# Hybrid decoder step on one core: the order of decode's loads on the SP queue

## The chip, the cores and the metric

The kernel runs on one core of a Trainium2 chip. The metric is the device time of one execution in microseconds (us); times of several executions are given by their median. The profiled execution is one more execution, recorded with a trace.

## The reference

One layer of a decoder is applied to a prompt of 512 tokens and to a decode batch of 8 sequences with 4 new tokens each. Each sequence of the decode batch has 1024 past tokens in a paged cache of 8 pages of 128 rows, found through `page_table`.

```python
yp, nsa_p, diff_p, win_p = decoder_layer(yp, p_nsa0, p_diff0, p_win0, ...)        # prompt
s_nsa  = cache_nsa_kv[l][page_table].reshape(DB, past_len, 4, 4, 64)              # k_cmp, v_cmp, k_sel, v_sel
s_diff = cache_diff_kv[l][page_table].reshape(DB, past_len, 2, 8, 128)            # keys (k1|k2), values
ys, nsa_s, diff_s, win_s = decoder_layer(ys, s_nsa, s_diff, s_win, ...)           # decode

# decoder_layer
proj = rmsnorm(x) @ w_in
o_a = nsa_mixer(...)     # 16 heads: compressed, selected and sliding branches, gated per head
a   = masked_softmax(q1 k1 + bias) - lam * masked_softmax(q2 k2 + bias)           # 8 heads
o_b = rmsnorm(a @ v) * (1 - lam_init)
h = x + (sigmoid(ga) * o_a + sigmoid(gb) * o_b) @ w_o
y = h + square(relu(rmsnorm(h) @ w_up)) @ w_down
```

## The kernel before

The program runs through five stages, each in a block of its own: projection, compression, prompt attention, decode attention (`decode_attention`, about 1008 to 1290 us in the trace) and the output projection with the MLP (`finish`). The change is in the loads of decode attention, and in the few of them that are issued while prompt attention still runs.

**Rounds.** Decode attention takes the 8 sequences in four rounds, `i` = 0 to 3 (`PAIRS` = 4), two sequences (a pair) in each. In a round TensorE (PE) turns key pages by transposes (`turn`), VectorE (DVE) or ScalarE (ACT) copies them out of PSUM into one of four slots, and PE multiplies them with the queries (`multiply`). `decode_steps` writes this order out as a list of steps. For a round it is: compressed keys (`cmp`), new rows, selected-branch pages (`sel`, 0 to 5), in rounds 1 to 3 the difference-attention values of the round before (`p_dif`, `p_dif_n`), `sel` 6 and 7, window pages (`win`), key pages of the difference attention (`dif`, each page k has four steps) 0 and 1, the values of the other branches (`p_sel`, `p_few`, `p_win`), and `dif` pages 2 to 7. In the last round all eight `dif` pages come ahead of the values. The values of the last round, `p_dif`, end the stage. So a value page of round i is read by PE some 10 us into round i + 1, while the list's key pages 4 to 7 are read at the end of round i. The list itself is not changed.

**Loads.** All large loads are issued by SP, in the order of its program, into one queue which the 16 DMA engines work off. SP also waits in that order: a wait in its program holds up all that stands behind it. For a pair there are, for both sequences together:

- `sel_load`: 8 pages, 2 x 256 KB each, into `big`. It waits until `nsa_mm` says that the values of the round before have been read
- `win_load`: 4 x 2 x 256 KB
- `key_load` (L204): 8 pages `dk`, 2 x 512 KB each, into four buffers (`KEY_PAGES`). Page k of round i goes where page k - 4 was, so `load_k` waits until the last of that page's four turns has been made (`turned`). The buffer of pages 0 and 4 is named `all_dk` in the profile, the others `de_dk`
- `load_v` (L1778): 8 pages `dv`, 2 x 512 KB each, into one buffer of eight pages. There is no second buffer, so round i's may be written only when PE has read round i - 1's
- `load_new` (L1765 to L1773), `pair_rows` (L177 to L179) and `dv_n` (L1797): new rows, compressed values `vc`, `gates`, queries and the like, together about 0.5 MB.

A page's place in the cache is a number in the table. `page_values` (L183) reads it into a register of SP: 16 reads for a pair. `sel`, `win` and the first `dk` page of pair 0 are loaded during prompt attention, which waits for `combined` before it may write `big` (L191).

Of the kernel before, what the change touches and what calls it, by code (L numbers as in the profile page):

```python
# [28 lines left out]
DEC_B, DEC_T = 8, 4  # L29
# [4 lines left out]
N_PAGES = PAST // PAGE  # L34
# [118 lines left out]
KEY_PAGES, KEYS_AHEAD = 4, 1  # L153
# [945 lines left out]
def prompt_attention(nc, d, shared):  # L1099


    with ExitStack() as ctx:
        s = Space(nc, ctx, "pa")
# [139 lines left out]
        def _(sp):  # L1243
# [28 lines left out]
            pages = page_values(sp, d, shared, 0)  # L1272

            sp.wait_ge(combined, NH)
            sel_load(sp, d, shared, pages, range(N_PAGES))
            win_load(sp, d, shared, 0)
            for k in range(KEYS_AHEAD):
                key_load(sp, d, shared, pages, 0, k)
# [349 lines left out]
def decode_attention(nc, d, shared):  # L1628


    with ExitStack() as ctx:
# [42 lines left out]
            shared.q_in, shared.kc_in, shared.sel_in, shared.win_in, shared.dk_in, shared.consts_in)  # L1674
        dv_in = [s.sem(f"dv_in{k}") for k in range(N_PAGES)]
# [85 lines left out]
        def _(sp):  # L1761
            def load_new(i):
# [5 lines left out]
                sp.dma_start(dk_n, split(d["diff_s"][new, 0:1024])).then_inc(new_in, 16)  # L1768
                sp.dma_start(vc[:], d["vc_s"][P * i:P * (i + 1), :]).then_inc(new_v_in, 16)
# [5 lines left out]

            def load_v(pages, i, k):
                for b in range(2):
                    sp.dma_start(dv[:, b, k, :], d["cache_diff"][bass.ds(pages[b][k], 1), :, 1024:2048]  # L1778
                                 .rearrange("n p e -> (n p) e")).then_inc(dv_in[k], 16)
# [9 lines left out]
            pages = page_values(sp, d, shared, 0)  # L1789
            for k in range(KEYS_AHEAD, KEY_PAGES):  # L1790
                load_k(pages, 0, k)
            for i in range(PAIRS):
                last = i + 1 == PAIRS
                if i:
                    sp.wait_ge(diff_mm, i)
                new = slice(2 * DEC_T * i, 2 * DEC_T * (i + 1))
                sp.dma_start(dv_n, d["diff_s"][new, 1024:2048].rearrange("(b t) e -> t b e", b=2)).then_inc(dv_n_in, 16)  # L1797
                load_v(pages, i, 0)
                load_v(pages, i, 1)
                if not last:  # L1800

                    sp.wait_ge(q_turned, i + 1)
                    sp.wait_ge(turned, AT[i, "cmp", 0, 0] + 1)
                    pair_rows(sp, d, shared, i + 1)
                load_v(pages, i, 2)
                load_v(pages, i, 3)
                load_k(pages, i, 4)
                load_v(pages, i, 4)
                load_k(pages, i, 5)
                load_v(pages, i, 5)  # L1810
                if not last:
                    following = page_values(sp, d, shared, i + 1)
                    sp.wait_ge(nsa_mm, i + 1)
                    sel_load(sp, d, shared, following, range(0, 3))
                    load_new(i + 1)
                load_k(pages, i, 6)
                if not last:
                    sel_load(sp, d, shared, following, range(3, 6))
                load_k(pages, i, 7)
                if not last:  # L1820
                    sel_load(sp, d, shared, following, range(6, 8))
                load_v(pages, i, 6)
                load_v(pages, i, 7)
                if not last:
                    win_load(sp, d, shared, i + 1)
                    for k in range(KEY_PAGES):
                        load_k(following, i + 1, k)
                    pages = following
# [22 lines left out]
        def _(pe):  # L1851
# [60 lines left out]
            def multiply(g):  # L1912
# [64 lines left out]
                elif kind == "p_dif":  # L1977
                    if i:
                        pe.wait_ge(diff_read, i)
                    for x in range(N_PAGES):  # L1980
                        pe.wait_ge(dv_in[x], 32 * i + 32)
                        for b in range(2):
                            for half in range(2):
                                o = 64 * b + 32 * half
                                ins = pe.matmul(ps_d[o:o + 32, :], tile[:, 64 * x + 32 * b:64 * x + 32 * b + 32],
                                                dv[:, b, x, CW * half:CW * (half + 1)], start=x == 0, stop=False)
                else:
# [820 lines left out]
```

## Time and profile before

| | us |
|---|---|
| three runs, median | 1776.53 |
| three runs, lowest and highest | 1768.65, 1789.45 |
| profiled execution, time | 1771.22 |
| profiled execution, span of the trace | 1769.4 |

The span runs from the first to the last instruction of the core; 1.8 us lie around it. Over the span PE is busy 92% of the time, DVE 45%, ACT 33% and GpSimd (POOL) 6%, and the mean granted clock of TensorE is 0.963 of full speed. The loads move 265.7 MB. Since the stages differ, the shares of the span say little about the loads of one of them; the rows further down are of the stage that the change touches.

### The profile page before, as it was taken

The page shows a single profiled execution, that of the slowest core. Times are in us where ns is not written, and L with a number is a line of the kernel's source. Part 1 is how long each engine was busy: PE and PEld are TensorE (multiplying, and loading weights), DVE is VectorE, ACT ScalarE, POOL GpSimd, SP SyncE. Part 2 cuts the span into 40 slices and gives each one's busy share as a digit, 9 for nine tenths or more (in the row PEclk, how much of TensorE's full clock was granted, in tenths as well). Part 3 has the DMA queues.
Part 4 walks back from the last instruction along what each step waited for, and adds up shares of the span by engine and source line. Part 5 has one row for each costly group of instructions (what it writes and reads, how often), then busy time and mean ns, then how long its engine had stood idle before and what let it go on. Part 6 is the DMA issues. An engine that isn't in the chain of part 4 may idle for free. (4 is left out here: it accounts for less than half of the span.)

```text
span 1769.4 us, 32753 instructions
## 1 busy us (share of the span) xinstructions
PE 1634.7 (92%) x12968; PEld 1360.4 (77%) x12968; DVE 804.9 (45%) x1873; ACT 586.8 (33%) x1236; POOL 106.0 (6%) x194
## 2 busy tenths in 40 slices
PE   7999999997899996788999888998979999999997
PEld 4888888775688885567777665765667999999997
DVE  4576633114233335867666544443454442234322
ACT  4232212222233324656555332332333332123210
POOL 0000000000000000035422100000000000000000
PEclk9999999998899998999999898998989999999999
DMA  8745555242532035542231089999842343333321
GB/s 279 294 163 169 161 162 161 91 137 51 137 78 73 8 97 151 140 145 69 89 116 31 17 322 361 364 337 341 325 159 72 95 132 111 113 115 121 97 71 51
DMA packets 187903, 265.71 MB, mean 150 GB/s; under 512 B 35261, under 2 KB 115517, under 8 KB 187654
## 3 DMA queue, kind: packets, MB, share of 16 engines
q1 hardware_dynamic: 183750, 244.31, 42.7%
q10 hardware_dynamic: 3136, 11.22, 1.7%
q0 software_dynamic: 896, 8.56, 1.4%
q8 instruction: 76, 1.25, 0.3%
q14 instruction: 45, 0.37, 0.1%
HBM read 240.98 MB, written 42.60 MB: 160 GB/s over the span
## 5 line engine op out<-in xcount | busy, mean ns | idle before, releaser
L614 PE MATMUL pj_ps<-all_hi,pj_xh 128*128 128x512 f32 x480 | 191.1, 398 | 1.5 <-DVE all_lo L508 1.5
L616 PE MATMUL pj_ps<-all_hi,pj_xl 128*128 128x512 f32 x480 | 189.5, 395 | 0.0
L615 PE MATMUL pj_ps<-all_lo,pj_xh 128*128 128x512 f32 x480 | 189.4, 395 | 0.0
L1424 ACT ACTIVATE pa_sc<-pa_sc,pa_nmax 128x32 f32<-128x32 f32 (+4 forms) x256 | 126.0, 493 | 115.0 <-DVE pa_nmax L1473 114.6
L2669 PE MATMUL fi_ps<-fi_fl,fi_wh 128*128 128x272 f32 x512 | 149.4, 292 | 0.0
L2670 PE MATMUL fi_ps<-fi_th,fi_wl 128*128 128x272 f32 x512 | 148.3, 290 | 0.0
L2670 PE MATMUL fi_ps<-fi_fh,fi_wl 128*128 128x272 f32 x512 | 148.3, 290 | 0.0
L2668 PE MATMUL fi_ps<-fi_th,fi_wh 128*128 128x272 f32 x512 | 147.6, 288 | 0.7 <-DVE fi_tl L2470 0.7
L2668 PE MATMUL fi_ps<-fi_fh,fi_wh 128*128 128x272 f32 x512 | 148.2, 289 | 0.0
L2669 PE MATMUL fi_ps<-fi_tl,fi_wh 128*128 128x272 f32 x512 | 147.2, 287 | 0.0
L2053 ACT ACTIVATE de_slot<-de_ps_t 128x512 f32<-128x512 f32 (+5 forms) x124 | 62.9, 514 | 188.1 <-PE de_ps_t L1888 98.4
L2165 DVE COPY de_slot<-de_ps_t 128x512 f32<-128x512 f32 (+4 forms) x112 | 68.8, 623 | 116.7 <-PE de_ps_t L1888 71.3
L1387 PE MATMUL pa_ps_t<-all_ident,pa_sc 128*128 128x128 f32 (+1 forms) x464 | 77.5, 285 | 36.0 <-DVE pa_keys L1481 12.6
L614 PEld LDWEIGHTS pj_ps<-all_hi,pj_xh 128*128 128x128 f32 x480 | 90.3, 188 | 25.4 <-issue 2.8
L1016 PE MATMUL cm_ph<-cm_xh,all_hi 128*128 128x512 f32 x256 | 108.4, 424 | 0.2 <-DVE cm_xl L880 0.2
L616 PEld LDWEIGHTS pj_ps<-all_hi,pj_xl 128*128 128x128 f32 x480 | 90.3, 188 | 21.4
L615 PEld LDWEIGHTS pj_ps<-all_lo,pj_xh 128*128 128x128 f32 x480 | 90.3, 188 | 20.8
L2396 ACT ACTIVATE fi_wh<-all_big 128x2048 fp32r<-128x2048 f32 x30 | 57.3, 1909 | 138.5 <-PE fi_ps L2670 138.5
L1017 PE MATMUL cm_ph<-cm_xl,all_hi 128*128 128x512 f32 x256 | 101.7, 397 | 0.0
L1018 PE MATMUL cm_ph<-cm_xh,all_lo 128*128 128x512 f32 x256 | 101.5, 396 | 0.0
L2668 PEld LDWEIGHTS fi_ps<-fi_fh,fi_wh 128*128 128x128 f32 x512 | 97.3, 190 | 0.0
L2670 PEld LDWEIGHTS fi_ps<-fi_fh,fi_wl 128*128 128x128 f32 x512 | 97.1, 190 | 0.0
(319 smaller groups left out, 3191.2 us busy)
## 6 DMA issues: line engine op xcount, KB each, us to landing
de_dv<-in_cache_diff SPq DMA_DIRECT2D x64, 512.0 KB, 10.5
all_big<-in_w_in SPq DMA_DIRECT2D x14, 2048.0 KB, 8.3
all_big<-in_cache_nsa SPq DMA_DIRECT2D x96, 256.0 KB, 5.6
de_dk<-in_cache_diff SPq DMA_DIRECT2D x48, 512.0 KB, 10.2
all_big<-in_w_up SPq DMA_DIRECT2D x16, 1024.0 KB, 5.5
all_big<-in_w_down SPq DMA_DIRECT2D x16, 1024.0 KB, 6.1
all_first<-in_cache_nsa SPq DMA_DIRECT2D x32, 256.0 KB
all_win<-in_cache_win SPq DMA_DIRECT2D x32, 256.0 KB, 10.7
```

The costliest lines, as they stand in the source:

```text
L614: pe.matmul(ps[:, t, :], xh[:, k, xk], hi(k), start=k == 0, stop=False)
L615: pe.matmul(ps[:, t, :], xh[:, k, xk], lo(k), start=False, stop=False)
L616: ins = pe.matmul(ps[:, t, :], xl[:, k, xk], hi(k), start=False, stop=k == KT - 1)
L1016: pe.matmul(o, w1h[k][:, kt, col], mh, start=first, stop=False)
L1017: pe.matmul(o, w1h[k][:, kt, col], ml, start=False, stop=False)
L1018: ins = pe.matmul(o, w1l[k][:, kt, col], mh, start=False, stop=last)
L1387: ins = pe.transpose(bank[0:r, P * k:P * (k + 1)], sc[:, x.n % 6, a, P * k:P * k + r], ident[:])
L1424: nc.scalar.activation(tile, tile, ACT.Exp, scale=-1.0, bias=nmax[:, x.n % 6, a:a + 1], accum_out=x.sums[a]).then_inc(probs, 1)
L2165: ins = nc.vector.tensor_copy(slot[rows, g % 4, cols], ps_t[rows, g % 4, cols])
L2668: pe.matmul(o, hi[:, k, :], a_hi[:, k, tok], start=k == 0, stop=False)
L2669: pe.matmul(o, hi[:, k, :], a_lo[:, k, tok], start=False, stop=False)
L2670: return pe.matmul(o, lo[:, k, :], a_hi[:, k, tok], start=False, stop=k == n_k - 1)
```

## The change

PE, DVE, ACT and POOL keep all their instructions in the same order. PE gets one increment more: after the four matmuls that read value page x (two for each sequence), it counts `dv_read` up by one. What moves is SP's program:

1. The page numbers of pairs 0 and 1 are read in prompt attention, ahead of the wait for `combined`, and kept. Decode attention no longer begins with a second reading of pair 0. The numbers of pair 2 and 3 are read when rounds 1 and 2 begin, ahead of `pair_rows`, and no longer between `dv` page 5 and the next `sel` pages.
2. A value page waits for its own page of the round before (`dv_read`), not for all of them and the new rows (`diff_mm`). All eight pages now stand ahead of the next pair's `sel` pages; pages 6 and 7 stood behind them. In the first three rounds six of them stand ahead of key page 4, where it was four.
3. `vc` and `gates` leave `load_new` for `load_new_v`, which comes later: behind key pages 1 to 3 in round 0, and behind the `sel` pages 3 to 5 after that. `dv_n` goes behind the eight value pages.
4. In the last round key pages 4 and 5 come behind four value pages, and 6 and 7 behind the fifth; the other three value pages come last.

```diff
             constant_loads(sp, d, shared)
             pair_rows(sp, d, shared, 0)
-            pages = page_values(sp, d, shared, 0)
+            shared.pages = [page_values(sp, d, shared, i) for i in range(2)]
 
             sp.wait_ge(combined, NH)
...
+            def load_dv_new(i):
                 if i:
                     sp.wait_ge(diff_mm, i)
                 new = slice(2 * DEC_T * i, 2 * DEC_T * (i + 1))
                 sp.dma_start(dv_n, d["diff_s"][new, 1024:2048].rearrange("(b t) e -> t b e", b=2)).then_inc(dv_n_in, 16)
...
+            def load_v(pages, i, k):
+                if i:
+                    sp.wait_ge(dv_read, N_PAGES * (i - 1) + k + 1)
...
+            load_new(0)
+            for k in range(KEYS_AHEAD, KEY_PAGES):
+                load_k(shared.pages[0], 0, k)
+            load_new_v(0)
+            for i in range(PAIRS - 1):
+                if i:
+                    shared.pages.append(page_values(sp, d, shared, i + 1))
+                pages, following = shared.pages[i:i + 2]
+                sp.wait_ge(q_turned, i + 1)
+                sp.wait_ge(turned, AT[i, "cmp", 0, 0] + 1)
+                pair_rows(sp, d, shared, i + 1)
+                for k in range(6):
+                    load_v(pages, i, k)
                 load_k(pages, i, 4)
-                load_v(pages, i, 4)
+                load_v(pages, i, 6)
                 load_k(pages, i, 5)
-                load_v(pages, i, 5)
-                if not last:
-                    following = page_values(sp, d, shared, i + 1)
-                    sp.wait_ge(nsa_mm, i + 1)
-                    sel_load(sp, d, shared, following, range(0, 3))
-                    load_new(i + 1)
+                load_v(pages, i, 7)
+                load_dv_new(i)
+                sp.wait_ge(nsa_mm, i + 1)
+                sel_load(sp, d, shared, following, range(0, 3))
+                load_new(i + 1)
                 load_k(pages, i, 6)
-                if not last:
-                    sel_load(sp, d, shared, following, range(3, 6))
+                sel_load(sp, d, shared, following, range(3, 6))
+                load_new_v(i + 1)
                 load_k(pages, i, 7)
-                if not last:
-                    sel_load(sp, d, shared, following, range(6, 8))
-                load_v(pages, i, 6)
-                load_v(pages, i, 7)
-                if not last:
-                    win_load(sp, d, shared, i + 1)
-                    for k in range(KEY_PAGES):
-                        load_k(following, i + 1, k)
-                    pages = following
+                sel_load(sp, d, shared, following, range(6, 8))
+                win_load(sp, d, shared, i + 1)
+                for k in range(KEY_PAGES):
+                    load_k(following, i + 1, k)
+            i, pages = PAIRS - 1, shared.pages[PAIRS - 1]
+            for k in range(4):
+                load_v(pages, i, k)
+            for k in (4, 5):
+                load_k(pages, i, k)
+            load_v(pages, i, 4)
+            for k in (6, 7):
+                load_k(pages, i, k)
+            for k in (5, 6, 7):
+                load_v(pages, i, k)
+            load_dv_new(i)
...
+                        ins.then_inc(dv_read, 1)
```

Two places of SP's program show it. In the rows below, L183 is a read of a page number (each with two register instructions behind it), and the ISA or REGISTER_ALU row ahead of a load forms its address.

First, the begin of decode attention. Before, from the load of the new keys on (16 reads in all stand between `gates` and the first key page):

```order
L1768 DMA de_new_rows<-out_diff_s 4x2x1024
L1769 DMA de_vc<-scratch_vc_s 128x256
L1773 DMA de_gates<-scratch_g 64x1x3 x2
L183 TENSOR_LOAD all_table
L183 ISA x2
```

After, from the load of the new keys on (the second half of key page 2 and page 3 are left out):

```order
L1769 DMA de_new_rows<-out_diff_s 4x2x1024
L204 ISA
L204 DMA de_dk<-in_cache_diff 128x1024
L204 ISA
L204 DMA de_dk<-in_cache_diff 128x1024
...
L1772 DMA de_vc<-scratch_vc_s 128x256
L1776 DMA de_gates<-scratch_g 64x1x3 x2
L177 DMA all_queries<-scratch_q 8x1024
```

The reads are gone from here, and `vc` and `gates` have moved behind the key pages.

Second, the end of a round's value pages in rounds 0 to 2, on SP. Before, key page 5 and value page 5, and then the reads for the next pair:

```order
L204 DMA de_dk<-in_cache_diff 128x1024
L1778 ISA
L1778 DMA de_dv<-in_cache_diff 128x1024
L1778 ISA
L1778 DMA de_dv<-in_cache_diff 128x1024
L183 TENSOR_LOAD all_table
L183 ISA x2
```

After, key page 5 and value page 7, and then the new value rows and the next pair's first `sel` page:

```order
L204 DMA de_dk<-in_cache_diff 128x1024
L1789 ISA
L1789 DMA de_dv<-in_cache_diff 128x1024
L1789 ISA
L1789 DMA de_dv<-in_cache_diff 128x1024
L1783 DMA de_new_rows<-out_diff_s 4x2x1024
L191 ISA
L191 DMA all_big<-in_cache_nsa 128x512
```

Nothing but the wait for `nsa_mm` now stands between the last value page and the `sel` pages, and two value pages more stand ahead of them.

## Rows read from the trace of the kernel before

**Rows 1.** Waits in decode: who waited for whom, us in total, times, longest

```profile
PE de_ps_t L1888 <- DMA de_dk<-in_cache_diff: 17.2, 8, 5.9
```

**Rows 2.** Timeline of PE in decode: start, us, line, operation, count, idle time before

```profile
1049.10 0.66 PE L1888 MATMUL de_ps_t<-all_ident,all_dk 128*128 128x128 f32 x4 [1.43 <-DMA all_dk<-in_cache_diff]
...
1054.31 0.66 PE L1888 MATMUL de_ps_t<-all_ident,de_dk 128*128 128x128 f32 x4 [1.79 <-DMA de_dk<-in_cache_diff]
...
1065.51 1.11 PE L1888 MATMUL de_ps_t<-all_ident,de_dk 128*128 128x128 f32 x4 [5.87 <-DMA de_dk<-in_cache_diff]
...
1072.10 0.66 PE L1888 MATMUL de_ps_t<-all_ident,de_dk 128*128 128x128 f32 x4 [0.61 <-DMA de_dk<-in_cache_diff]
...
1085.71 7.07 PE L1985 MATMUL de_ps_d<-de_dv,de_slot 128*32 128x512 f32 x64
...
1116.05 1.08 PE L1960 MATMUL de_ps_n<-all_win,de_slot 128*32 128x128 f32 x32
...
1138.19 1.09 PE L1888 MATMUL de_ps_t<-all_ident,de_dk 128*128 128x128 f32 x8 [2.91 <-DMA de_dk<-in_cache_diff]
...
1152.31 7.05 PE L1985 MATMUL de_ps_d<-de_dv,de_slot 128*32 128x512 f32 x64
...
1198.83 1.11 PE L1888 MATMUL de_ps_t<-all_ident,de_dk 128*128 128x128 f32 x4 [1.74 <-DMA de_dk<-in_cache_diff]
...
1206.77 0.66 PE L1888 MATMUL de_ps_t<-all_ident,de_dk 128*128 128x128 f32 x4 [2.06 <-DMA de_dk<-in_cache_diff]
...
1222.39 7.07 PE L1985 MATMUL de_ps_d<-de_dv,de_slot 128*32 128x512 f32 x64
...
1250.98 1.09 PE L1888 MATMUL de_ps_t<-all_ident,all_dk 128*128 128x128 f32 x8
...
1254.18 1.09 PE L1888 MATMUL de_ps_t<-all_ident,de_dk 128*128 128x128 f32 x8
...
1259.18 1.09 PE L1888 MATMUL de_ps_t<-all_ident,de_dk 128*128 128x128 f32 x8 [1.74 <-DMA de_dk<-in_cache_diff]
...
1277.97 7.78 PE L1985 MATMUL de_ps_d<-de_dv,de_slot 128*32 128x512 f32 x64
```

**Rows 3.** Stretches of decode: length, busy time of each engine, PE's clock, DMA share, GB/s

```profile
1021.60:1090.00 68.40, 58.46 (x870) 43.37 (x866) 28.57 (x82) 18.97 (x39) 1.25 (x2) 0.93 1.01 373
1090.00:1138.00 48.00, 43.91 (x662) 32.83 (x654) 22.76 (x61) 14.80 (x29) 3.34 (x6) 0.93 0.93 332
1138.00:1160.00 22.00, 21.81 (x261) 13.58 (x262) 8.15 (x25) 6.40 (x13) 0.00 (x0) 0.92 1.04 401
1160.00:1207.00 47.00, 41.77 (x631) 31.79 (x630) 22.80 (x63) 15.31 (x29) 3.33 (x6) 0.93 0.92 327
...
1065.00:1070.00 5.00, 4.49 (x40) 3.38 (x44) 1.11 (x2) 0.60 (x1) 0.00 (x0) 0.50 1.04 398
```

**Rows 4.** Timeline of SP's queue: start, us, line, load, count

```profile
748.23 0.35 SPq L179 DMA_DIRECT2D all_kc<-scratch_kc_s  x1
...
777.00 9.66 SPq L191 DMA_DIRECT2D all_big<-in_cache_nsa  x16
...
1009.86 2.29 SPq L1773 DMA_DIRECT2D de_gates<-scratch_g  x2
1021.57 3.25 SPq L204 DMA_DIRECT2D de_dk<-in_cache_diff  x6
...
1068.32 7.78 SPq L198 DMA_DIRECT2D all_win<-in_cache_win  x8
...
1077.63 3.92 SPq L204 DMA_DIRECT2D de_dk<-in_cache_diff  x6
1093.83 0.30 SPq L1797 DMA_DIRECT2D de_new_rows<-out_diff_s  x1
```

**Rows 5.** Waits of SP's queue over the whole run, the first load of decode

```profile
SPq L191 <- DVE pa_ob L1506: 18.9, 1, 18.9
```

**Rows 6.** Timeline of DVE in round 0: the first reader of the gates

```profile
1031.55 0.16 DVE L2210 TENSOR_TENSOR de_rr<-de_rr,de_gates 128x3 f32<-128x3 f32 x1
```

More of the change, by code:

```diff
@@ L1271, in _ @@
             pair_rows(sp, d, shared, 0)
-            pages = page_values(sp, d, shared, 0)
+            shared.pages = [page_values(sp, d, shared, i) for i in range(2)]
             sp.wait_ge(combined, NH)
-            sel_load(sp, d, shared, pages, range(N_PAGES))
+            sel_load(sp, d, shared, shared.pages[0], range(N_PAGES))
             win_load(sp, d, shared, 0)
             for k in range(KEYS_AHEAD):
-                key_load(sp, d, shared, pages, 0, k)
+                key_load(sp, d, shared, shared.pages[0], 0, k)
             sp.wait_ge(o_sq, 1)
@@ L1674, in decode_attention @@
             shared.q_in, shared.kc_in, shared.sel_in, shared.win_in, shared.dk_in, shared.consts_in)
+        dv_read = s.sem("dv_read")
         dv_in = [s.sem(f"dv_in{k}") for k in range(N_PAGES)]
@@ L1768, in load_new, with load_new_v @@
                 sp.dma_start(dk_n, split(d["diff_s"][new, 0:1024])).then_inc(new_in, 16)
+            def load_new_v(i):
                 sp.dma_start(vc[:], d["vc_s"][P * i:P * (i + 1), :]).then_inc(new_v_in, 16)
@@ L1774, in load_new @@
                                      d["g"][at:at + DEC_T, :].rearrange("t (h c) -> h t c", c=3)).then_inc(new_v_in, 16)
+            def load_dv_new(i):
+                if i:
+                    sp.wait_ge(diff_mm, i)
+                new = slice(2 * DEC_T * i, 2 * DEC_T * (i + 1))
+                sp.dma_start(dv_n, d["diff_s"][new, 1024:2048].rearrange("(b t) e -> t b e", b=2)).then_inc(dv_n_in, 16)
             def load_v(pages, i, k):
+                if i:
+                    sp.wait_ge(dv_read, N_PAGES * (i - 1) + k + 1)
                 for b in range(2):
@@ L1788, in _ @@
             load_new(0)
-            pages = page_values(sp, d, shared, 0)
             for k in range(KEYS_AHEAD, KEY_PAGES):
-                load_k(pages, 0, k)
-            for i in range(PAIRS):
-                last = i + 1 == PAIRS
+                load_k(shared.pages[0], 0, k)
+            load_new_v(0)
+            for i in range(PAIRS - 1):
                 if i:
[L1795 to L1799, printed above, removed]
-                if not last:
[L1802 to L1806, printed above, removed]
+                    shared.pages.append(page_values(sp, d, shared, i + 1))
[5 more added lines that the diff above has]
+                    load_v(pages, i, k)
@@ L1822, in _ @@
-                load_v(pages, i, 6)
-                load_v(pages, i, 7)
-                if not last:
-                    win_load(sp, d, shared, i + 1)
-                    for k in range(KEY_PAGES):
-                        load_k(following, i + 1, k)
-                    pages = following
+                sel_load(sp, d, shared, following, range(6, 8))
+                win_load(sp, d, shared, i + 1)
+                for k in range(KEY_PAGES):
+                    load_k(following, i + 1, k)
```

## Prediction

> **What bounds the kernel now.** I read the waits of decode first. PE waits there for hardly anything but key pages: eight times for `de_dk`, 17.2 us in all [rows 1], and once, 1.43 us, for the page in `all_dk` [rows 2]. The timeline of PE says where: 1.43, 1.79, 5.87 and 0.61 us before key pages 4 to 7 of round 0, 2.91 us before page 7 of round 1 (one of 0.5 us, the rest of the eight, lies just ahead of it), 1.74 and 2.06 us before pages 6 and 7 of round 2, 1.74 us before page 6 of the last round [rows 2]. The reader should also see what a wait leaves behind: the granted clock is 0.50 in the stretch after the 5.87 us, the lower of its two levels, 1.2 GHz [rows 3]. Undisturbed, a key page takes 3.2 us from start to start (1250.98 to 1254.18); page 6 of round 0 took 6.59 with 0.61 of waiting in it, so 2.8 us went to the clock [rows 2].
>
> Then the stretches: from 1021.6 to 1090 the DMA engines are busy at a share of 1.01, so the late pages are late because the queue is full, not because SP is slow to ask. At 401 GB/s a full queue (share 1.04) moves a pair's 22 MB of pages (23.1 million bytes) in 57.5 us, against 66.7 and 70.1 us from one `p_dif` to the next [rows 2, 3]. In 1090 to 1138 and 1160 to 1207 the shares are 0.93 and 0.92: about 48 x 0.11 / 1.04 = 5.1 us and 47 x 0.12 / 1.04 = 5.4 us of transfer time are not used there [rows 3]. And the queue starts late: SP is done with `gates` at 1012.15 and issues its first key page only at 1021.57 [rows 4]. Nothing is loaded in between; the 16 page numbers are read, 9.4 us, 0.59 us each.
>
> **The change, part by part.** I follow key page 7 of each round, the last that PE waits for.
>
> *Start of the queue.* The 9.4 us of reads and the 2.7 us of issuing `vc` and `gates` (1009.46 to 1012.15) leave the way of key pages 1 to 3: the queue begins 12.1 us earlier. The reads go to prompt attention. There SP issues at 748.23 for 0.35 us, waits 18.9 us in all and goes on at 777.00 [rows 4, 5]; 16 reads fill the remaining 9.5 us, and 16 more fit into the 18.9. Cost nothing; without that cover the `sel` pages would be 9.4 us late at 777, and PE doesn't want them before decode.
>
> *vc and gates later.* In round 0 they now queue behind 3.1 MB, 8 us by 401 GB/s, and land near 1022; DVE wants `gates` at 1031.55 [rows 6]. Nothing waits. They add their transfer to what stands ahead of the keys: page 5's start at 1054.31 to page 6's at 1065.51 is 11.2 us for 3.67 MB that take 9.2, so 2 us belong to `load_new` with both of these; I count 1 us.
>
> *Two value pages more ahead of key pages 6 and 7.* 2.1 MB, +5.2 us for each of them in every round, once against the old order, since the queue's total stays the same.
>
> *Round 0.* Key page 7 could be used at 1072.10; now at 1072.1 - 12.1 + 5.2 + 1 = 1066.2. Without any wait PE would want it 1.43 + 1.79 + 5.87 + 0.61 + 2.8 = 12.5 us earlier than in the trace, at 1059.6. The queue is later, so it decides: **5.9 us gained**, and `p_dif` of pair 0 starts at 1079.8 instead of 1085.7.
>
> *Round 1.* The queue carries the same -5.9, plus what it regains of the unused 5.1. What opened that gap goes: value pages waited for all of `p_dif` (first one issued after 1093.83), and 9.4 us of reads stood ahead of the `sel` pages. The reads now stand at the round's begin. SP's last key issue ended at 1081.55 while the transfers kept on at a full share to 1090 at least [rows 3, 4], since issuing was itself held back (7.78 us for the 2.1 MB of `win`, which transfer in 5.2). So the reads are covered by some 10 us of backlog, and they are over about when the first value page comes free. A new gap: the wait for `nsa_mm` (end of the `win` values, 1117.1, 31.4 us after `p_dif` [rows 2]) now falls at 1111.2, while ten pages (2.6 us each) and 3 us of small loads stand behind the round's last key page, which is through near 1083.5 (1066.2 and 7.3 MB behind key page 7, 18.3 us, less a us since a page can be used only some time after its transfer): 1112.5. The two times are about equal, and I count 1 us. Key page 7: 1138.2 - 5.9 - 4.1 = 1128.2. PE wants it at 1138.2 - 5.9 - 3.4 = 1128.9. PE decides, by a hair: 9.3 us gained. Of what the lower clock costs after a wait (2.8 us in round 0, and the wait here was half as long) I count 0.7 us as gone too. **10 us** by `p_dif` of pair 1 (1142.3).
>
> *Round 2.* Queue: -5.9, regained 10.5 less a gap of 1 and one of 2.6, -12.8 in all: 1194.0. The 2.6 are an estimate. The queue is near dry again as `nsa_mm` comes (1142.3 + 31.4 = 1173.7), and SP issues `sel` loads no faster than they transfer (9.66 us for 16, 0.6 us for 256 KB [rows 4]), so its issues for `vc` and `gates` between them lie bare. PE without waits: 1206.8 - 10 - 1.74 - 2.06 - 2.7 (page 6 at the lower clock, 5.9 for 3.2) = 1190.3. The queue decides: **12.8 us**.
>
> *Last round.* Keys 6 and 7 have one value page ahead of them instead of two, and the queue is 12.8 us earlier; the 1.74 us go. The value pages behind come 13 us earlier than they did, and `p_dif` reads them last. **14.5 us** at 1277.97, and all that follows moves with it. Increments of `dv_read` cost PE nothing that I can name: the matmuls of a page take 0.9 us (7.07 / 8) and other matmuls of the stage carry such increments already.
>
> Sum: 14.5 us. The profiled execution would go from 1771.2 to 1756.7. The three runs and the profiled one lie at 1768.7, 1771.2, 1776.5 and 1789.5, their middle is 1773.9, 2.7 over the profiled one and 2.6 under the median of three. I take that middle as the base: **1759.4 us**. About 1% (18 us) is what a measurement of this kernel can tell from no change.
>
> **The rivals.**
>
> *PE decides everywhere.* If the queue is ahead by key page 6 of round 0 (the small loads may cost less than I count, the 16 engines may not need strict order), all waits go: 12.5 + (3.4 + 1.5) + (3.8 + 2.7 + 1.5) + 1.7 = 27.1 us, 1746.8. The 1.5 us are an estimate, half of the 2.8, for the clock after the last wait of rounds 1 and 2. For it: the queue has 12 us of head start and uses 57.5 us of every 62 that PE then needs. Against it: the two value pages ahead of keys 6 and 7 in round 0, where nothing can be regained, as the share is 1.01 already.
>
> *The engines don't reach their full rate in the rounds.* Over 1090 to 1138 and 1160 to 1207 they averaged 332 and 327 GB/s [rows 3]. Should that be the small loads' doing (rows of new tokens, `gates` of 12 bytes a piece) and not idle time, the gaps stay; each key page 7 is then 5.9 us early, as in round 0, and the last round adds 1.7: 7.6 us, 1766.3. Against it: 373 GB/s in the first stretch, with the same small loads in it. The Trainium skill speaks for it (DMA: Bandwidth & Descriptors, "Where 436 GB/s comes from"): for transfers from HBM the memory's side binds, at about 358 GB/s for a core; by that figure the two value pages cost 5.9 us and a pair's pages 64 us, more than PE needs for a round, and the gain would be some 7 us. This trace disagrees: 22 us at 401 GB/s.
>
> *The reads run the queue dry, slower than before.* This decides if the backlog at the last key issue is under 9.4 us: value pages, keys and `sel` pages all stand behind the reads on SP. With none of it the queue loses 9.4 us in round 1 and again in round 2, and some 1.5 us at each restart, against -5.9 and the 10.5 of the old gaps: 2 x 10.9 - 5.9 - 10.5 = 5.4, less the last round's 1.7: +3.7 us, 1777.6. For it: the queue runs ahead of PE more often now, and then the backlog shrinks. Against it: 1081.55 and the full share to 1090; and where PE is the one behind, the value pages aren't free earlier anyhow.
>
> *The change does nothing.* Only if SP were late for the `sel` pages in prompt attention; the 18.9 us exclude it.
>
> **How the numbers follow.** Forecast (10 to 19 us gained) 0.57; PE decides (19 to 28) 0.18; rate stays low (3 to 10) 0.17; slower 0.08. More than 1% faster: all but a little of the second, and the upper end of the first with the scatter of the runs, 0.3. More than 1% slower needs that rival and bad luck in the runs: 0.04. The range takes in the PE-bound case and the low-rate one with a few us of scatter: 1745 to 1771.
>
> **What would show it.** First key page on SP's queue near 1009.5, not 1021.6. In round 0 waits for key page 4 and 5 gone, page 6 2 to 4 us, page 7 under 1. `p_dif` at about 1080, 1142, 1210 and 1263. DMA share over 1.0 from 1012 to 1100 and small dips at the `nsa_mm` waits. Wrong: waits on `de_dv` or `gates`, a share under 0.9 while SP reads numbers, or `p_dif` of pair 0 before 1076 or after 1083.

## The result, and the profile after

Over 20 runs of each kernel the median went from 1777.8 to 1767.7 us; the ratio of the times is 0.9933 (95% interval 0.9911 to 0.9954), about 12 us or 0.7% faster. The forecast was 1759.4: 8.3 us too low, 3.9 of them because my base of 1773.9 from four executions lay under the 1777.8 of twenty, 4.3 because the gain was 10.2 between medians and not 14.5. In decode itself the profiles show 9.1 to 9.4 us.

The profiled execution of the changed kernel took 1778.3 us, more than the one of before (1771.2). Decode begins 19 us later in it, at 1027.6 instead of 1008.6. So whole executions don't compare here, stages do. Two lengths serve below: decode as a whole, from the first matmul of `turn_queries` to the end of the last matmuls on new value rows (1285.68 + 1.06 - 1008.60 = 278.1 us before, 269.0 after), and its rounds, cut at the starts of `p_dif`. The expectations count decode to the start of that last group, 1.1 us less.

The waits of decode, changed kernel (line L1898 is the L1888 of before); it answers to [rows 1]:

```profile
PE de_ps_t L1898 <- DMA de_dk<-in_cache_diff: 11.5, 6, 4.7
```

The timeline of PE, changed kernel, at the places of [rows 2]. Times less 19.0 compare with those of before:

```profile
1027.63 2.35 PE L2016 MATMUL de_ps_n<-all_ident,all_queries 8*64 8x8 f32 x32 [6.60 <-PEq L96]
...
1062.36 1.08 PE L1970 MATMUL de_ps_n<-all_win,de_slot 128*32 128x128 f32 x32
...
1077.37 0.66 PE L1898 MATMUL de_ps_t<-all_ident,de_dk 128*128 128x128 f32 x4 [1.61 <-DMA de_dk<-in_cache_diff]
...
1084.44 0.66 PE L1898 MATMUL de_ps_t<-all_ident,de_dk 128*128 128x128 f32 x4 [2.15 <-DMA de_dk<-in_cache_diff]
...
1099.61 7.07 PE L1995 MATMUL de_ps_d<-de_dv,de_slot 128*32 128x512 f32 x64
...
1128.39 1.08 PE L1970 MATMUL de_ps_n<-all_win,de_slot 128*32 128x128 f32 x32
...
1144.03 1.09 PE L1898 MATMUL de_ps_t<-all_ident,de_dk 128*128 128x128 f32 x8 [1.45 <-DMA de_dk<-in_cache_diff]
...
1152.02 1.97 PE L1898 MATMUL de_ps_t<-all_ident,de_dk 128*128 128x128 f32 x8 [4.72 <-DMA de_dk<-in_cache_diff]
...
1166.81 7.05 PE L1995 MATMUL de_ps_d<-de_dv,de_slot 128*32 128x512 f32 x64
...
1198.20 1.08 PE L1970 MATMUL de_ps_n<-all_win,de_slot 128*32 128x128 f32 x32
...
1212.34 1.12 PE L1898 MATMUL de_ps_t<-all_ident,de_dk 128*128 128x128 f32 x4 [0.74 <-DMA de_dk<-in_cache_diff]
...
1219.25 0.66 PE L1898 MATMUL de_ps_t<-all_ident,de_dk 128*128 128x128 f32 x4 [0.82 <-DMA de_dk<-in_cache_diff]
...
1233.36 7.07 PE L1995 MATMUL de_ps_d<-de_dv,de_slot 128*32 128x512 f32 x64
```

Key pages 4 and 5 of round 0 are on time now, and the last round waits for nothing. But pages 6 and 7 are late in every round, and in round 1 the wait for page 7 is longer than before (4.72 against 2.91 us). The three rows with `all_win` carry what I hadn't read. They are the matmuls of the window values (`p_win`), and with their end PE counts up `nsa_mm`, the semaphore that SP waits for ahead of the next pair's `sel` pages. I write `nsa_mm` for that time. Page 6 is used 13.9, 14.6 and 13.1 us after it and page 7 21.0, 22.5 and 20.0 us after it. In the kernel before it was 14.3 and 21.1 us in round 1 (1117.1 to 1131.4 and 1138.2 [rows 2]), 14.0 and 22.0 in round 2; only round 0 stood apart (21.9 and 28.4), where the queue began late and was still full of earlier loads.

SP's timeline, changed kernel, round 1, behind `nsa_mm` at 1129.5:

```profile
1129.68 4.44 SPq L191 DMA_DIRECT2D all_big<-in_cache_nsa  x6
...
1135.38 0.90 SPq L204 DMA_DIRECT2D de_dk<-in_cache_diff  x2
1136.48 5.01 SPq L191 DMA_DIRECT2D all_big<-in_cache_nsa  x6
...
1143.38 0.95 SPq L204 DMA_DIRECT2D de_dk<-in_cache_diff  x2
```

The same place of the kernel before, behind `nsa_mm` at 1117.1:

```profile
1119.05 3.09 SPq L191 DMA_DIRECT2D all_big<-in_cache_nsa  x6
...
1125.07 0.96 SPq L204 DMA_DIRECT2D de_dk<-in_cache_diff  x2
...
1130.61 1.05 SPq L204 DMA_DIRECT2D de_dk<-in_cache_diff  x2
```

In the changed kernel SP issues key page 6 5.9 us after `nsa_mm` and page 7 13.9 us after it, because six and twelve `sel` loads (three and six pages) and the small ones stand ahead in its program. In the kernel before it was 7.9 and 13.5 us; there SP came to the wait 1.9 us late, out of the page numbers' reads. The stretches of the DMA engines, changed kernel, show the hole:

```profile
1031.10:1090.00 58.90, 54.89 (x800) 42.55 (x799) 28.34 (x83) 17.66 (x36) 1.25 (x2) 0.89 1.02 380
1090.00:1152.00 62.00, 54.95 (x846) 39.90 (x838) 29.32 (x85) 19.10 (x40) 3.32 (x6) 0.98 0.96 346
...
1130.00:1140.00 10.00, 10.00 (x169) 7.80 (x168) 5.34 (x10) 3.58 (x6) 1.03 (x2) 1.00 0.84 237
```

The same place before the change:

```profile
1115.00:1130.00 15.00, 15.00 (x254) 11.71 (x256) 7.26 (x19) 4.58 (x8) 1.04 (x2) 0.98 0.88 296
```

237 GB/s for the 10 us behind `nsa_mm` against the 401 of [rows 3] is 4.1 us of transfer time not used; 296 GB/s over 15 us is 3.9 us. Counted by busy share, as the prediction did, the two are 10 x 0.20 / 1.04 = 1.9 and 15 x 0.16 / 1.04 = 2.3 us: part of the hole is idle time, the rest is busy engines that move fewer bytes. Either way the gap wasn't closed. Over whole rounds the share went from 0.96 to 0.97 in round 1 and stayed at 0.96 in round 2. In round 0 there was no such hole: the share was 1.04 from `nsa_mm` to the use of key page 7 (1063.4 to 1084.4).

### The profile page after: what moved, and what is told of

It reads as the page before. It is cut to its first block and busy times, and to the rows that moved or that the text cites. A ratio compares the mean times of both kernels' runs of the same rounds, so it can differ in the third digit from the quotient of the medians.

```text
span 1776.5 us, 32705 instructions
## 1 busy us (share of the span) xinstructions
PE 1651.5 (93%) x12968; PEld 1372.7 (77%) x12968; DVE 802.3 (45%) x1873; ACT 587.3 (33%) x1236; POOL 105.8 (6%) x194
## 5 line engine op out<-in xcount | busy, mean ns | idle before, releaser
L2064 ACT ACTIVATE de_slot<-de_ps_t 128x512 f32<-128x512 f32 (+5 forms) x124 | 62.8, 513 | 177.2 <-PE de_ps_t L1898 87.3
L2176 DVE COPY de_slot<-de_ps_t 128x512 f32<-128x512 f32 (+4 forms) x112 | 68.7, 622 | 106.3 <-PE de_ps_t L1898 61.7
L1387 PE MATMUL pa_ps_t<-all_ident,pa_sc 128*128 128x128 f32 (+1 forms) x464 | 81.4, 296 | 32.7 <-DVE pa_keys L1481 12.3
L1387 PEld LDWEIGHTS pa_ps_t<-all_ident,pa_sc 128*128 128x128 f32 (+1 forms) x464 | 51.5, 143 | 59.2 <-issue 16.2
L2679 PEld LDWEIGHTS fi_ps<-fi_th,fi_wh 128*128 128x128 f32 x512 | 96.4, 188 | 0.8 <-DVE fi_tl L2481 0.8
```

Source lines behind the costliest of these rows:

```text
L1387: ins = pe.transpose(bank[0:r, P * k:P * (k + 1)], sc[:, x.n % 6, a, P * k:P * k + r], ident[:])
L2176: ins = nc.vector.tensor_copy(slot[rows, g % 4, cols], ps_t[rows, g % 4, cols])
L2679: pe.matmul(o, hi[:, k, :], a_hi[:, k, tok], start=k == 0, stop=False)
```

## The experiments

Measured lengths, all from one profile each (rounds in us; the last column is the ratio of the run's time to the kernel before, with its interval):

| kernel | round 0 | 1 | 2 | last | rest | decode | ratio |
|---|---|---|---|---|---|---|---|
| before | 77.1 | 66.6 | 70.1 | 55.6 | 8.8 | 278.1 | |
| before, once more (12) | 75.8 | 67.0 | 70.4 | 56.4 | 9.9 | 279.5 | |
| changed | 72.0 | 67.2 | 66.5 | 53.8 | 9.5 | 269.0 | 0.9933 (0.9911 to 0.9954) |
| changed, once more (11) | 73.1 | 66.3 | 69.1 | 53.1 | 8.5 | 270.1 | |
| 1 before, reads kept | 72.4 | 67.2 | 70.0 | 57.0 | 9.2 | 275.7 | 0.9962 (0.9928 to 0.9997) |
| 2 changed, reads back | 79.8 | 63.3 | 70.0 | 52.1 | 8.0 | 273.2 | 0.9998 (0.9962 to 1.0034) |
| 3 value pages 6, 7 behind | 71.5 | 64.9 | 66.5 | 52.0 | 8.0 | 263.0 | 0.9927 (0.9889 to 0.9966) |
| 4 key page 6 ahead of the wait | 66.2 | 60.5 | 66.5 | 52.0 | 8.1 | 253.2 | 0.9861 (0.9816 to 0.9906) |
| 5 value pages wait for all | 73.2 | 68.7 | 69.1 | 52.9 | 8.0 | 271.9 | 0.9920 (0.9891 to 0.9949) |
| 6 reads behind six value pages | 72.6 | 64.7 | 68.0 | 52.9 | 8.0 | 266.2 | 0.9942 (0.9912 to 0.9972) |
| 7 last round's old order | 71.9 | 64.7 | 68.5 | 53.8 | 9.8 | 268.6 | 0.9949 (0.9911 to 0.9986) |
| 8 before, with 4's order of keys | 73.6 | 58.9 | 67.4 | 58.1 | 9.5 | 267.5 | 0.9919 (0.9884 to 0.9953) |
| 9 both key pages ahead of the wait | 64.7 | 59.6 | 64.7 | 54.0 | 9.2 | 252.2 | 0.9827 (0.9790 to 0.9863) |
| 10 4 and 6 together | 66.6 | 62.8 | 65.2 | 52.0 | 8.1 | 254.7 | 0.9844 (0.9814 to 0.9873) |

How far to trust a length: the two profiles of the same kernel differ by 1.4 and 1.1 us in decode and by up to 2.6 in a round. Under 3 us in decode I read nothing into a difference. The ratios rest on 6 to 10 runs of each edited kernel, on three chips, each with runs of the kernel before on the same chip.

**1. Before, with the numbers of pair 0 kept**

```
-            pages = page_values(sp, d, shared, 0)                    # in prompt attention
+            pages = shared.pages0 = page_values(sp, d, shared, 0)
...
-            pages = page_values(sp, d, shared, 0)                    # in decode attention
+            pages = shared.pages0
```

> The kernel before with one edit: decode attention keeps the page numbers of pair 0 that prompt attention read, instead of reading them a second time (16 reads, 9.4 us on SP). Order of the loads, waits and places of the other reads are the old ones. Length of decode (from the first matmul of turn_queries to the last group of new value rows) was 277.1 us before and 267.9 after the whole change. Theory A (all that the change gains is the head start of the queue; the gaps of rounds 1 and 2 are not closed by it): every key page 7 comes 9.4 us earlier, decode takes about 268, as short as with the whole change, and the run is 9 us faster than before. Theory B (page-wise values and moved reads bring a good part of it): decode takes 272 or more, at most 5 us gained.

Measured: decode 275.7, a gain of 2.4 to 3.8 us, and 4.7 by `p_dif` of pair 0 (or 3.4). Theory A, my first after the result, falls. The PE timeline of this kernel shows what took the place of the old waits in round 0:

```profile
1063.84 1.11 PE L1888 MATMUL de_ps_t<-all_ident,de_dk 128*128 128x128 f32 x4 [2.57 <-DMA de_dk<-in_cache_diff]
...
1070.52 1.11 PE L1888 MATMUL de_ps_t<-all_ident,de_dk 128*128 128x128 f32 x4 [1.79 <-DMA de_dk<-in_cache_diff]
```

`nsa_mm` is at 1048.95 there (1047.87 + 1.08): 14.9 and 21.6 us again, with a queue 9 us ahead of the old one. From this came the chain theory: once the queue has worked off what was asked for before `nsa_mm`, a round is paced by `nsa_mm` and by what stands between it and key pages 6 and 7 on SP.

**2. Changed, with pair 0's reads back at decode's begin**

```
             load_new(0)
+            shared.pages[0] = page_values(sp, d, shared, 0)
```

> The changed kernel with pair 0's 16 page numbers read once more at the begin of decode, ahead of key pages 1 to 3; all else as changed. Theory A: the head start falls from 12.1 to 2.7 us, decode goes from 267.9 back to 275 to 278, the time of the kernel before. Theory B: the rest of the change keeps 4 us or more, decode takes 273 or less. A third reading, that the queue has slack at the start, leaves it at 268.

Measured: decode 273.2 (272.1 in the expectation's count), as Theory B had it. Round 0 is 79.8, longer than before the change: there the queue is behind again and value pages 6 and 7 do stand ahead of the keys (page 7 29.7 us after `nsa_mm`). The rest of the change keeps some 5 us in the profile, in round 1 and the last; the time of the runs doesn't show them (0.9998), and its interval doesn't exclude them. By the runs the head start weighs more than by the profiles: with it alone 0.9962, with all but it 0.9998, with all 0.9933, and the intervals of the last two don't touch. One profile of each kernel can't settle that.

**3. Value pages 6 and 7 behind key page 7**

```
                 load_k(pages, i, 4)
-                load_v(pages, i, 6)
                 load_k(pages, i, 5)
-                load_v(pages, i, 7)
                 load_dv_new(i)
...
                 sel_load(sp, d, shared, following, range(6, 8))
+                load_v(pages, i, 6)
+                load_v(pages, i, 7)
```

> The changed kernel with value pages 6 and 7 issued behind key page 7 and the sel pages 6 and 7, as before, in rounds 0 to 2. By the 5.2 us that these two pages cost as a term of the prediction, key page 7 of round 0 comes 5 us earlier and PE waits there no more; decode 260 to 264 by Theory A. If the term was wrong (the queue makes up for it otherwise), decode stays at 267 to 269. Should the value pages then come too late for p_dif, PE waits for de_dv and decode gets longer.

Measured: decode 263.0, 6 us less (7 against the second profile) and in the range of the expectation, but not the way that was expected. In round 0 key page 7 isn't 5 us earlier: PE waits 3.69 us for it, 20.5 us after `nsa_mm`, and the round is as long as in the changed kernel (71.5 against 72.0). So with the head start the 5.2 us of these pages aren't on the path of round 0. They turned into idle time instead: in the 5 us ahead of `nsa_mm` (1051.5) and the 5 us behind it the DMA share is 0.82 and 0.68, where the changed kernel has 1.02 and 1.03. The profile gains 2.3 us in round 1, 1.7 in the last and 1.5 in the rest, each within the scatter of a round; their sum is over the 3 us, and where it comes from stays open. The time of the runs is that of the changed kernel (0.9927 against 0.9933).

**4. Key page 6 ahead of the wait for `nsa_mm`**

```
                 load_dv_new(i)
+                load_k(pages, i, 6)
                 sp.wait_ge(nsa_mm, i + 1)
                 sel_load(sp, d, shared, following, range(0, 3))
+                load_k(pages, i, 7)
                 load_new(i + 1)
-                load_k(pages, i, 6)
                 sel_load(sp, d, shared, following, range(3, 6))
                 load_new_v(i + 1)
-                load_k(pages, i, 7)
                 sel_load(sp, d, shared, following, range(6, 8))
```

> The changed kernel with key page 6 issued ahead of the wait for nsa_mm and key page 7 behind the first three sel pages; load_new behind key page 7. The sel pages come 2.6 us later. In the changed kernel's profile PE waits 1.61 and 2.15 us in round 0, 1.45 and 4.72 in round 1, 0.74 and 0.82 in round 2 for these two pages, and about 4 us more go to the lower clock. Theory A (order decides: what stands ahead of the two keys is late, what stands behind is not wanted yet): all of that goes, decode 253 to 258, the run 8 us or more faster than the changed kernel. Theory C (the queue's total rate binds): the waits move to the sel or win pages of the next round, decode 265 to 268.

Measured: decode 253.2, ratio 0.9861. The same bytes, the same waits, and 16 us less than the changed kernel in decode. The PE timeline of this kernel, the only DMA waits of decode:

```profile
1080.79 0.66 PE L1898 MATMUL de_ps_t<-all_ident,de_dk 128*128 128x128 f32 x4 [1.10 <-DMA de_dk<-in_cache_diff]
...
1142.28 1.09 PE L1898 MATMUL de_ps_t<-all_ident,de_dk 128*128 128x128 f32 x8 [1.71 <-DMA de_dk<-in_cache_diff]
...
1205.78 1.11 PE L1898 MATMUL de_ps_t<-all_ident,de_dk 128*128 128x128 f32 x4 [2.92 <-DMA de_dk<-in_cache_diff]
```

All three are for page 7, 16.6, 18.0 and 18.4 us after `nsa_mm`; page 6 is never late. No wait moved to the `sel` or `win` pages, so the queue's total rate isn't what held the changed kernel at its rounds of 67 us (Theory C falls).

The end of `p_win` on PE and SP's next loads, in round 1 of this kernel, say what the edit did and what it didn't:

```profile
1123.18 1.08 PE L1970 MATMUL de_ps_n<-all_win,de_slot 128*32 128x128 f32 x32
...
1125.44 0.84 SPq L204 DMA_DIRECT2D de_dk<-in_cache_diff  x2
1126.51 3.74 SPq L191 DMA_DIRECT2D all_big<-in_cache_nsa  x6
1130.43 0.84 SPq L204 DMA_DIRECT2D de_dk<-in_cache_diff  x2
```

Key page 6 stands ahead of the wait in the program, but it is issued 1.2 us behind `nsa_mm` (1124.3), and 1.0 us behind it in rounds 0 and 2. It has a wait of its own: it goes where page 2 was, and PE makes the last turn of page 2 about as it comes to `nsa_mm`. Page 7 follows 6.0 to 6.2 us behind `nsa_mm`. So the wait itself costs next to nothing here; what the edit takes away is the loads between it and the two keys. And the queue is now at its limit: the DMA share is 1.03 at 385 GB/s over round 1, 1.02 at 384 over round 2. At 385 GB/s a pair's 23.1 MB take 60.0 us, and round 1 lasts 60.5.

**5. Value pages wait for all of the round before**

```
-                if i:
-                    sp.wait_ge(dv_read, N_PAGES * (i - 1) + k + 1)
+                if i and k == 0:
+                    sp.wait_ge(dv_read, N_PAGES * i)
```

> The changed kernel with the value pages of a round waiting together until PE has read all eight of the round before (some 6 us later than the first one now). Two theories by now. Chain theory: a round is paced by the wait for nsa_mm, since key pages 6 and 7 stand behind it and behind three and six sel pages on SP; they are used 13 to 15 and 20 to 22 us after nsa_mm in every round so far, whatever the queue did ahead of it. Then value pages that come 6 us later change little, since they have 23 us until nsa_mm: decode 268 to 271 in rounds of 67, unless p_dif or key pages 4 and 5 come to wait. Queue theory (my prediction's: the round's total of transfers decides): each of three rounds gets longer by up to 6 us, decode 275 or more.

Measured: decode 271.9, 1.8 to 2.9 us more than the changed kernel, about the scatter, and no difference in the time of the runs (0.9920). The 6 us by which value pages come later reach PE only in part, and in one round: in round 1 pages 6 and 7 are used 17.5 and 24.7 us after `nsa_mm`, so the queue reached into it there. The page-wise wait is worth 0 to 1 us a round here.

**6. The reads behind value pages 0 to 5**

```
-                if i:
-                    shared.pages.append(page_values(sp, d, shared, i + 1))
-                pages, following = shared.pages[i:i + 2]
+                pages = shared.pages[i]
...
                 for k in range(6):
                     load_v(pages, i, k)
+                if i:
+                    shared.pages.append(page_values(sp, d, shared, i + 1))
+                following = shared.pages[i + 1]
                 load_k(pages, i, 4)
```

> The changed kernel with the page numbers of pairs 2 and 3 read behind value pages 0 to 5 of rounds 1 and 2, where SP waits for key page 4's buffer anyhow, and not at the round's begin. Chain theory: no change, decode 267 to 270, since nsa_mm sets the pace. Queue theory: 1 us or more gained in each of the two rounds, decode 264 to 266.

Measured: decode 266.2, 2.8 and 3.9 us under the two profiles of the changed kernel, at the edge of the scatter, and 0.9942 in the runs. In the expectation's count it is 265.1, in the range of the queue theory and under that of the chain theory. Inconclusive between "nothing" and "1 us a round"; experiment 10 comes back to it. It excludes that the reads at the round's begin run the queue dry at a high price, as the slower rival had it.

**7. The last round in its old order**

```
             for k in (4, 5):
                 load_k(pages, i, k)
-            load_v(pages, i, 4)
+                load_v(pages, i, k)
             for k in (6, 7):
                 load_k(pages, i, k)
-            for k in (5, 6, 7):
+            for k in (6, 7):
                 load_v(pages, i, k)
```

> The changed kernel with the last round's loads in the old order: value page 5 ahead of key pages 6 and 7. The last round had one DMA wait before the change (1.74 us for key page 6) and none after. If the order removed it, it comes back with 1 to 2 us, decode 270 to 271; if the earlier queue did, decode stays at 268 to 269.

Measured: last round 53.8 with one wait of 0.17 us, against 53.8 and 53.1 in the changed kernel. The new order of the last round does nothing that can be seen; so the 1.74 us of before went with the rest of the change, the earlier queue.

**8. Before, with experiment 4's order of the keys**

```
                 if not last:
                     following = page_values(sp, d, shared, i + 1)
+                load_k(pages, i, 6)
+                if not last:
                     sp.wait_ge(nsa_mm, i + 1)
                     sel_load(sp, d, shared, following, range(0, 3))
-                    load_new(i + 1)
-                load_k(pages, i, 6)
-                if not last:
-                    sel_load(sp, d, shared, following, range(3, 6))
                 load_k(pages, i, 7)
                 if not last:
-                    sel_load(sp, d, shared, following, range(6, 8))
+                    load_new(i + 1)
+                    sel_load(sp, d, shared, following, range(3, 8))
```

> The kernel before, with the order of experiment 4 alone: key page 6 ahead of the wait for nsa_mm, key page 7 behind the first three sel pages, load_new behind it. Reads, waits and value pages are the old ones, so there is no head start. Chain theory: rounds 1 and 2 fall from 66.6 and 70.1 us to 60 to 64, and round 0, where the full queue decides, gains the 4 to 5 us of the sel pages and small loads that no longer stand ahead of key page 7; decode 262 to 266 instead of 278, better than the whole change. Queue theory: the transfers still have to be made, the waits move into the next round's sel and win pages; decode 273 or more.

Measured: decode 267.5 (266.4 in the count of the expectation, just above the 262 to 266 of the chain theory), ratio 0.9919. Nothing of the change is in this kernel, and it is as fast as the whole change (0.9933), by another way: round 1 falls from 66.6 to 58.9, round 0 by 3.5. Round 2 is at 67.4 with 2.49 us of waiting for page 7, and the last round got 2.5 us longer (waits of 0.71 and 1.95). The DMA share is 1.02 and 1.03 over rounds 1 and 2: the queue is full there too.

**9. Both key pages ahead of `nsa_mm`**

```
                 load_dv_new(i)
+                load_k(pages, i, 6)
+                load_k(pages, i, 7)
                 sp.wait_ge(nsa_mm, i + 1)
```

> The changed kernel with both key pages, 6 and 7, ahead of the wait for nsa_mm; the sel pages, load_new and load_new_v behind it. In experiment 4, where only page 6 stood ahead, PE waited 1.10, 1.71 and 2.92 us for page 7 and nothing for page 6. Chain theory: these waits and the slow clock behind them go, rounds of 60 to 61, decode 246 to 250; the sel pages come some 5 us later, and if they are what is late next, PE waits for all_big or all_win and decode stays at 253 or gets longer.

Measured: decode 252.2, ratio 0.9827, the lowest of all, 1751.1 against 1781.1 us of the kernel before on that chip. Decode (251.1 in the expectation's count) is above the 246 to 250 of the chain theory and below the 253 of its alternative. The waits for page 7 are gone; in round 1 PE waits once for something new, 0.81 us for the rows that `load_new` brings, and in round 2 0.37 and 0.46 us for key pages 5 and 6. Again the first of the two keys is issued 1.0 us behind `nsa_mm` (1061.41 against 1060.45), so nothing leaves ahead of it. The DMA share is 1.03 over round 1: what is late next is in sight, and the 1 us less than in experiment 4 is inside the scatter.

**10. Experiment 4's order with experiment 6's reads**

> Experiment 4's order of the keys with the reads of experiment 6 (page numbers of pairs 2 and 3 read behind value pages 0 to 5). With shorter rounds the queue is closer to its limit, so value pages and keys held up by 9 us of reads may count now where they didn't: 1 to 2 us in rounds 1 and 2, decode 250 to 252, if the queue is what makes page 7 late in experiment 4; unchanged at 253 if it is the three sel pages ahead of it.

Measured: decode 254.7, ratio 0.9844. Page 7 still waits 2.50 and 1.62 us in rounds 1 and 2. So the place of the reads isn't what makes page 7 late in experiment 4. Experiment 9, which takes the three `sel` pages from ahead of it, ends those waits. Experiment 6's gain of 2.8 us has no counterpart here (254.7 against 253.2): I take it for scatter.

**11 and 12. Both kernels once more**

> The changed kernel once more, for the scatter of a profile: decode was 269.0 us, and kernels that differ from it only in the last round or the place of the reads had rounds 1 that differ by up to 2.6 us. All theories expect 266 to 271. It also tells whether the late begin of decode in its profile (1027.6 against 1008.6 us) is the kernel's or that execution's.

> The kernel before once more, for the scatter of a profile: all theories expect a decode of 276 to 280 us and a begin of decode between 1008 and 1028 us. A begin near 1008 again would speak for a cost of the 16 more reads in prompt attention; a later one against it.

Measured: decode 270.1 and 279.5 us, so the gain in decode is 9.1 and 9.4 us. Decode begins at 1023.1 and 1014.7. In round 1 of this second profile of the kernel before, pages 6 and 7 are used 16.3 and 23.0 us after `nsa_mm`, so the 14 and 21 us aren't fixed to better than 2 us.

## Why the prediction held, and where it didn't

The time came out inside the range and near the sum, but for reasons that hold only in part: the term for round 1 failed, and that of round 0 was right in size alone.

**Start of the queue.** The reads in prompt attention are hidden, as said: SP's wait there (L191) fell from 18.9 to 11.9 us and no more of it was needed. The first key page is issued 1.0 us after decode's first matmul instead of 13.0, 12 us of head start as worked out.

**Round 0.** Forecast 5.9 us gained, measured 5.1 (2.7 between the second profiles). Page 7 was used 56.8 us into decode, where the sum by the queue had put it at 57.6. The number held, the reason didn't: it was put down to the queue's bytes, with 5.2 us for value pages 6 and 7, and experiment 3 takes these away and leaves page 7 where it was. `nsa_mm` comes at 35.8 us, and 21 us behind it is 56.8. With this order of the loads behind `nsa_mm` the head start can hardly bring more, since `nsa_mm` comes out of PE's own work. In the changed kernel's profile the engines are also full over those 21 us (1.04); that the queue isn't what sets the time there rests on experiment 3.

**Rounds 1 and 2: the step that failed.** The prediction had the queue regain 4.1 and 2.8 us of its unused time and a new gap of 1 to 2.6 us at `nsa_mm`. Measured at key page 7 the kernel is 5.2 us ahead in round 1 and 6.6 in round 2 (forecast 9.3 and 12.8; 3.4 and 5.9 between the second profiles). Round 1 itself gained nothing: it is 0.6 us longer in the first pair of profiles and 0.7 shorter in the second, where 4.1 had been forecast. Round 2 gained 3.6 and 1.3 us for a forecast of 2.8. The mechanism was misread. I took `nsa_mm` for a short gap in a queue that its total decides; the chain that starts at it is the pace. In the changed kernel SP has nothing to issue for 7 us until it comes (1122.2 to 1129.7 in round 1), and then issues three `sel` pages and small loads ahead of key page 6 and three more ahead of page 7. The pages are used some 14 and 21 us after it in both kernels (13 to 16 and 20 to 23 in rounds 1 and 2 of the four profiles), while PE wants them some 12 to 13 and 16 us after it. A round is then 30 to 33 us from `p_dif` to `nsa_mm`, 20 to 23 to page 7 and 14 to 16 to the next `p_dif`. Experiments 4, 8 and 9 show that the order behind `nsa_mm` counts, by moving little but the keys: -16 and -17 us in decode against the changed kernel (4 and 9), -11 against the one before (8). What they don't show is a round without the wait: the two keys' own buffers come free about 1 and some 4 us behind `nsa_mm`, as PE turns pages 2 and 3, and no order on SP can bring them before that. The measured course is nearest to the rival "the rate stays low", which had each page 7 early by 5.9 us and 1766.3 as the time; but its cause, the engines' rate with small loads, isn't it, or experiment 4 couldn't have run its round 1 in 60.5 us at 385 GB/s with the same loads.

**Last round.** Its wait went, 1.7 us, as forecast; the reason given (fewer value pages ahead) was wrong in part, by experiment 7.

**The rivals.** PE decides in none of the first three rounds, but the 27 us that this rival promised are nearly reached by a kernel that asks for its keys in time: experiments 4 and 9 gain 25 and 26 us in decode. The reads don't run the queue dry at the price of that rival (experiments 6 and 10); its 1.5 us for each restart stands on no row, and no run here measured one. The changed kernel runs at 380 GB/s over 59 us, small loads included. The rule of the Trainium skill that memory binds at about 358 GB/s (DMA: Bandwidth & Descriptors, "Where 436 GB/s comes from"), a core's half of what two share, isn't borne out by that on this one core.

**The signs.** First key page at 1009.6 on the clock of before (forecast 1009.5); waits for pages 4 and 5 of round 0 gone; page 6 waits 1.6 us (forecast 2 to 4) and page 7 2.2 (forecast under 1). `p_dif` comes at 1080.6, 1147.8, 1214.4 and 1268.1, for a forecast of 1080, 1142, 1210 and 1263: right once, then 6, 4 and 5 us late. One slip in the working: the first of the two distances between `p_dif` is 66.6 us, not 66.7; nothing hangs on it.

**What stays open.** By the profiles, experiments 1 and 2 give the head start 2 to 4 us of decode and the rest of the change 5 to 7; by the times of the runs the head start is 7 to 12 us and the rest 0 to 5. The two don't agree, and which holds is not settled. Nor is which part of the rest counts, the page-wise wait (at most 3) or the place of the reads in rounds 1 and 2 (none at first sight), nor why rounds with the same waits differ by 3 us.

## What to carry to other kernels

When a load is late, look up not only how full the queue is, but when the issuing engine reached it and which wait it came out of: a time from that wait to the use that stays nearly the same, round after round and in both kernels, points at what is issued behind the wait, and work done ahead of it can't shorten it. Order the loads behind a wait by when they are wanted. Before you expect a load to leave ahead of the wait, look up what it waits for itself: key page 6 stood ahead of `nsa_mm` in experiments 4 and 9 and still left 1 us behind it. A head start is worth only what the next such wait lets through.

## What the runs showed of the hardware that I had not expected

The begin of decode, so the stages ahead of it, scatters by up to 20 us between profiles: 1008.6, 1012.1, 1013.3 and 1014.7 in the four with 16 reads in prompt attention, 1014.5 to 1028.2 in the ten with 32. The means are 1012.2 and 1022.2. The same kernel differs by 6.1 us (before) and 4.5 (changed). From the first `sel` load to decode's first matmul it was 231.6 us in the profile of before and 242.6 in that of the changed kernel, at a granted clock of 0.96 against 0.88 in 790 to 1000 us. Two of the kernels with 32 reads (experiments 2 and 3) took 229.8 and 231.6 us there, so the reads don't fix it; whether they make a long stretch more frequent isn't settled. Nor does the clock alone explain it: experiment 4 took 241.7 us at 0.94. The times of the runs leave little room for a cost: they fell by 10 to 12 us where decode fell by 9.

Two value pages (2.1 MB) more or less ahead of a late key moved nothing where a wait of the issuing engine lay between (experiment 3, round 0: 20.5 against 21.0 us after `nsa_mm`), although the DMA engines were at a share of 1.02 over that stretch (1031.1 to 1090) in the changed kernel.
